# Gate groups placed between the up-projection tiles of PEER from tile 60 on, with its routing run first

## What is computed

```python
def peer(x, w_query, sub_keys, expert_u, expert_v):          # H = 8 heads, K = 16
    q = (xt @ w_query).reshape(T, H, 2, PEER_KEY_DIM // 2)
    s = jnp.einsum('thpd,hpnd->thpn', q, sub_keys)            # scores on 2 x 128 sub-keys
    sv, si = lax.top_k(s, K)
    cand = (sv[:, :, 0, :, None] + sv[:, :, 1, None, :]).reshape(T, H, K * K)
    cidx = (si[:, :, 0, :, None] * PEER_N_KEYS + si[:, :, 1, None, :]).reshape(T, H, K * K)
    best, pos = lax.top_k(cand, K)
    eidx = jnp.take_along_axis(cidx, pos, axis=-1)
    gate = jax.nn.softmax(best, axis=-1)
    a = jnp.einsum('chkd,cd->chk', expert_u[eidx], x)
    w = gate * gelu(a)
    y = jnp.einsum('chk,chkd->cd', w, expert_v[eidx])
```

## Time and profile before

| | |
|---|---|
| median of 3 runs | 2197.05 us (2192.01 to 2198.41) |
| span of the profiled execution | 2194.3 us |
| TensorE busy | 97% of the span |
| VectorE, ScalarE, GpSimd busy | 68%, 53%, 8% |
| up-projection, layer 0 | from 291.6 to 664.6 us |
| gate stage, layer 0 | from 664.6 to 746.3 us |
| down-projection, layer 0 | from 746.3 to 1097.3 us |

### The profile page before, as it was taken

One profiled execution on the slowest core, in us unless ns is written; L12 is line 12 of the kernel. 1 busy time (PEld: TensorE's weight loads), 2 busy tenths in 40 slices (PEclk: granted clock), 3 DMA queues, 4 the chain that ended last, 5 costly groups with the idle time before them and its releaser, 6 DMA issues.

```text
span 2194.3 us, 41496 instructions
## 1 busy us (share of the span) xinstructions
PE 2136.5 (97%) x14244; PEld 1917.2 (87%) x14244; DVE 1500.2 (68%) x2796; ACT 1156.8 (53%) x1835; POOL 181.5 (8%) x202
## 2 busy tenths in 40 slices
PE   8999999999999999999999999999999999999997
PEld 6987899999997788888788888999999977888886
DVE  6666767777778855555676566777777797555556
ACT  4456445544458755445444464444544596444443
POOL 1100000000007400000020000000000182000000
PEclk9999999999999999999999999999999999999999
DMA  5622455555550256666565234555555503665664
GB/s 187 198 86 88 155 165 182 182 183 183 182 180 27 59 191 193 201 203 198 160 197 167 88 106 154 166 183 183 183 183 182 166 0 101 195 201 191 200 204 134
DMA packets 97584, 350.24 MB, mean 160 GB/s; under 512 B 11312, under 2 KB 11344, under 8 KB 97520
## 3 DMA queue, kind: packets, MB, share of 16 engines
q1 hardware_dynamic: 94320, 338.69, 48.3%
q0 software_dynamic: 3200, 10.66, 1.6%
HBM read 348.26 MB, written 1.05 MB: 159 GB/s over the span
## 4 chain that ended last, share of the span: by engine, by line
PE 85%; DMA 4%; DVE 4%; ACT 2%; issue 2%; POOL 1%; POOLq 0%; DVEq 0%; SPq 0%; ACTq 0%
PE wide L1536 33%; PE acc L1521 13%; PE acc L1522 13%; PE acc L1523 13%; PE acc L2003 4%; DMA raw<-in_front 2%; DMA raw<-in_peer_v 2%; PE tr L1714 1%; POOL hot_i L574 1%; ACT hot_i L844 1%; PE acc L1874 1%; ACT hi L601 1%; PE acc L1876 1%; PE acc L1875 1%; PE wide L1972 1%
## 5 line engine op out<-in xcount | busy, mean ns | idle before, releaser
L601 ACT ACTIVATE hi<-raw 128x1024 fp32r<-128x1024 f32 (+1 forms) x644 | 676.3, 1051 | 540.7 <-DMA raw<-in_peer_v 341.9
L919 DVE TENSOR_TENSOR lo<-raw,hi 128x1024 fp32r<-128x1024 f32 x520 | 636.8, 1225 | 448.6 <-ACT hi L601 445.6
L1521 PE MATMUL acc<-xT_hi,lo 128*128 128x256 f32 x2544 | 724.9, 285 | 5.9 <-DVE kr L1132 3.2
L1522 PE MATMUL acc<-xT_lo,hi 128*128 128x256 f32 x2544 | 721.1, 283 | 0.0
L1523 PE MATMUL acc<-xT_hi,hi 128*128 128x256 f32 x2544 | 721.0, 283 | 0.0
L1521 PEld LDWEIGHTS acc<-xT_hi,lo 128*128 128x128 f32 x2544 | 489.4, 192 | 12.6 <-issue 4.6
L1522 PEld LDWEIGHTS acc<-xT_lo,hi 128*128 128x128 f32 x2544 | 489.6, 192 | 0.0
L1523 PEld LDWEIGHTS acc<-xT_hi,hi 128*128 128x128 f32 x2544 | 489.5, 192 | 0.0
L1536 PE MATMUL wide<-hi,w_lo 128*128 128x512 f32 x1016 | 313.9, 390 | 5.4 <-DVE w_lo L1462 5.2
L1536 PE MATMUL wide<-lo,w_hi 128*128 128x512 f32 x1016 | 312.9, 389 | 0.0
L1536 PE MATMUL wide<-hi,w_hi 128*128 128x512 f32 x1016 | 312.8, 389 | 0.0
(11 more groups left out here) (307 smaller groups left out, 1943.2 us busy)
## 6 DMA issues: line engine op xcount, KB each, us to landing
raw<-in_peer_u SPq DMA_DIRECT2D x256, 512.0 KB, 3.5
raw<-in_peer_v SPq DMA_DIRECT2D x254, 512.0 KB, 3.5
raw<-in_front SPq DMA_DIRECT2D x114, 512.0 KB, 3.5
ln_par<-in_ln POOLq DMA_DIRECT2D x10, 512.0 KB, 5.6
raw<-in_front SPq DMA_DIRECT2D x12, 384.0 KB, 3.2
w<-in_cmp_w POOLq DMA_DIRECT2D x16, 256.0 KB, 4.3
raw<-in_front SPq DMA_DIRECT2D x8, 312.0 KB, 3.4
xs<-in_x SPq DMA_DIRECT2D x2, 512.0 KB, 4.6
```

The costliest lines, as they stand in the source:

```text
L601: nc.scalar.activation(hi[:, s, :width], raw[:, s, :width], ACT.Identity).then_inc(hi_done, 1)
L919: nc.vector.tensor_tensor(lo[:, s], raw[:, s], hi[:, s].bitcast(F32), ALU.subtract).then_inc(lo_done, 1)
L1521: mm(dst, lo[:, s, c], xh[:, k], start=k == 0, stop=False)
L1522: mm(dst, hi[:, s, c], xl[:, k], start=False, stop=False)
```

## The change

The gate stage is taken apart and laid into the second half of the up-projection. `G0` is 60.

- TensorE runs tiles 0 to 59, with the transposes of the picks after tiles 57 and 58, then for m = 0 to 63: tile 60 + m and gate group m (into `tr` instead of `acc`), then tiles 124 to 127. `apart_j` and `v_half` are gone.
- GpSimd makes the low parts of tiles 3 to 59 (57 tiles, 128x1024 each). Its differences are gone.
- VectorE does the 16 routing units one behind the other with nothing between (24 instructions each, as the copy of the scores into `r_s`, L1346, is gone). Then it makes the rows of groups 0 and 1 and the low parts of tiles 60 to 62. For each m it then multiplies the Gelu of tile 60 + m into `big`, makes the rows of group m + 2 (8 instructions of 128x128, with iota against the token's pick), multiplies the gates of group m into all of `big`, and makes the low part of tile 63 + m.
- ScalarE writes the Gelu of tiles from 60 on into two buffers (`acts`), and fills the part of `big` behind tile 59 with ones in 34 pieces: one after each of the tiles 8 to 33, 36, 37, 40, 41, 44, 45, 56 and 57. The pieces at 36, 40 and 44 lie over the scores and wait for routing unit 4, 8 and 12 to be done. After tile 56 it waits for the end of the routing and takes the exponential of the gates.

The core of the diff:

```diff
@@ gpsimd
-                def differences(i, e):
-                    ...
+                for k in range(POOL_FIRST, G0):
+                    n = T_U + k
+                    s = n % SLOTS
+                    pool.wait_ge(hi_done, l * NT + n + 1)
+                    nc.gpsimd.tensor_tensor(lo[:, s], raw[:, s], hi[:, s].bitcast(F32), ALU.subtract).then_inc(pool_lo, 1)
@@ scalar
+                def gelu_tile(k):
+                    n = T_U + k
+                    tile_used(l, n // SLOTS, n % SLOTS)
+                    if k < G0:
+                        dst = big[:, k // JB, :, k % JB]
+                    else:
+                        if k >= G0 + 2:
+                            act.wait_ge(tile_times, l * N_TIMES + k - G0 - 1)
+                        dst = acts[k % 2][:].rearrange("p (g t) -> p g t", t=TB)
+                    ...
+                ones_at = {8 + h: h for h in range(N_ONES - 8)}
+                for c in range(3):
+                    for half in range(2):
+                        ones_at[36 + 4 * c + half] = N_ONES - 8 + 2 * c + half
+                after_gelu(0)
+                for k in range(NKEYS):
+                    gelu_tile(k)
+                    if k > 0:
+                        after_gelu(k)
+                    if k in ones_at:
+                        if ones_at[k] >= N_ONES - 8:
+                            unit_done = 4 * ((ones_at[k] - (N_ONES - 8)) // 2 + 1)
+                            act.wait_ge(route_step, (l * 16 + unit_done) * ROUTE_STEPS)
+                        fill_ones(ones_at[k])
+                    if k == 56:
+                        act.wait_ge(best_ready, l + 1)
+                        nc.scalar.activation(picks[:, 2], picks[:, 2], ACT.Exp).then_inc(gate_exp, 1)
+                        fill_ones(N_ONES - 2)
+                    ...
@@ vector
-                after_route(0, 0)
-                route(0, 0, (1, 2, 3))
-                with dve.Fori(0, NKEYS // 8 - 2) as i:
-                    route(i + 1, i, range(4, 12))
-                route(NKEYS // 8 - 1, NKEYS // 8 - 2, range(4, 11))
+                for i in range(TT * HEADS):
+                    route(i)
+                def rows(m):
+                    if m >= 2:
+                        dve.wait_ge(gates_out, l * NG + m - 1)
+                    for r in range(4):
+                        t = 4 * m + r
+                        nc.vector.tensor_scalar(hot_i[:, m % 2, r], iota[:], picksT[:, 0, t:t + 1], None, ALU.is_equal)
+                        ins = nc.vector.tensor_scalar(hot_j[:, m % 2, r], iota[:], picksT[:, 1, t:t + 1], picksT[:, 2, t:t + 1],
+                                                      ALU.is_equal, ALU.mult)
+                    ins.then_inc(hot_ready, 1)
+                ...
+                rows(0)
+                rows(1)
+                dve.wait_ge(ones_done, (l + 1) * N_ONES)
+                for k in range(G0, G0 + AHEAD):
+                    split_of(k)
+                for m in range(NG):
+                    if m > 0:
+                        dve.wait_ge(gates_read, 2 + l * NG + m)
+                    times_tile(G0 + m)
+                    if m + 2 < NG:
+                        rows(m + 2)
+                    times_gates(m)
+                    split_of(G0 + m + AHEAD)
@@ tensor
+                def gates_of(i, e):
+                    pe_.wait_ge(hot_ready, l * NG + (i * 8 + (e + 1)))
+                    pe_.wait_ge(gates_read, l * NG + (i * 8 + (e + 1)))
+                    for r in range(4):
+                        ins = mm(tr[:, e % 2, r * P:(r + 1) * P], hot_i[:, e % 2, r], hot_j[:, e % 2, r], start=True, stop=True)
+                    ins.then_inc(gates_out, 1)
+                ...
+                for k in range(56, G0):
+                    u_tile(k)
+                    if k == 57:
+                        pe_.wait_ge(best_ready, l + 1)
+                        transpose_heads(X_PK, [picks[:, a, tt] for a in range(2) for tt in range(TT)], P)
+                    if k == 58:
+                        pe_.wait_ge(picks_ready, l + 1)
+                        transpose_heads(X_PK + 1, [picks[:, 2, tt] for tt in range(TT)], P)
+                with pe_.Fori(0, NG // 8) as i:
+                    for e in range(8):
+                        u_tile_of(i, G0, e)
+                        gates_of(i, e)
+                for k in range(G0 + NG, NKEYS):
+                    u_tile(k)
```

More of the change, by code:

```diff
@@ new lines, in fill_ones, with after_gelu @@
+                def fill_ones(half):
+                    a, part = divmod(half, 2)
+                    dst = big[:, G0 // JB + a, 32 * part:32 * part + 32].rearrange("p g j t -> p (g j t)")
+                    nc.scalar.activation(dst.rearrange("p (b i) -> p b i", i=P), iota[:].unsqueeze(1).broadcast_to([P, 4, P]),
+                                         ACT.Identity, bias=ones[:, 0:1], scale=0.0).then_inc(ones_done, 1)
+                def after_gelu(k):
+                    n = T_U + k + AHEAD
+                    split_hi(l, n // SLOTS, n % SLOTS)
@@ L1373, in route @@
-                    assert sum(map(len, stages)) == ROUTE_STEPS
-                    split_after = [round((len(stages) - 1) * (e + 0.5) / len(splits)) for e in range(len(splits))]
-                    for g, stage in enumerate(stages):
-                        for ins in stage:
-                            rt.mark(ins())
-                        for e in splits:
-                            if split_after[e - splits[0]] == g:
-                                after_route(turn, e)
-                        rt.settle()
@@ L1382, in route @@
[L1382 to L1392 removed]
+                    for p in range(2):
+                        rt.mark(nc.vector.max(r_v[:, p, 0:8], scores[p]))
@@ L1523, in columns_tile @@
                     ins = mm(dst, hi[:, s, c], xh[:, k], start=False, stop=k == DK - 1)
-                    if part is not None and k == 3:
-                        ins.then_inc(part, 1)
                 ins.then_inc(slot_free[s], 1)
@@ L1980, in _ @@
+                for k in range(8):
+                    u_tile(k)
+                with pe_.Fori(0, 6) as i:
                     for e in range(8):
-                        u_tile(i, e)
-                for e in range(8):
-                    u_tile(NKEYS // 8 - 1, e, quarter_read if e == 7 else None)
-                    if e == 4:
+                        u_tile_of(i, 8, e)
+                for k in range(56, G0):
+                    u_tile(k)
+                    if k == 57:
                         pe_.wait_ge(best_ready, l + 1)
@@ L2006, in step @@
-                def step(i, nxt, fresh=False):
-                    for e in range(HOTS):
-                        gates_of(i, e)
-                        if nxt is not None:
-                            apart_j(*nxt, e, fresh)
-                half = NG // HOTS // TT
-                step(FIRST, (0, 1))
-                with pe_.Fori(1, half - 1) as i:
-                    step(i, (0, i + 1))
-                step(half - 1, (1, 0), True)
-                with pe_.Fori(half, 2 * half - 1) as i:
-                    step(i, (1, i - (half - 1)))
```

377 lines of the change are left out of this document (127 added, 250 removed).

## The result

The changed kernel takes 2303.23 us (median of 4 runs, 2299.9 to 2306.5) against 2196.24 us beside it: ratio 1.0486, 95% interval 1.0469 to 1.0503. It is 4.9% slower. The prediction said 2280, range 2205 to 2345. The profiled execution has a span of 2304.8 us against 2194.3.

What follows compares the result with a forecast made beforehand. TensorE, 97% busy, was taken as the bound. A 66 us loss less 23.6 gained is 42.4 a layer, 85 for both: 2194.3 + 85 = 2279, 2282 with 2.75 for the median; forecast 2280 us, range 2205 to 2345.

Steps and rivals of the forecast that it cites:

- The forecast's case: Routing beside GpSimd: eight VectorE instructions a unit wait for GpSimd's whole instruction, stalling TensorE; 2280 us, chance 0.50.
- eight contenders: VectorE instructions in each routing unit, three with two SBUF inputs and five small, each waiting 0.92 us on average for GpSimd.
- The rival in which only three contend: Routing: only the instructions with two SBUF inputs wait, the five small ones don't; unit 12.6 us, about 2226 us, chance 0.20.
- the hidden routing: Rival: blocking by GpSimd is rare, routing ends at 159 us and fits behind TensorE's work; 2154 us, chance 0.12.
- The rival of unchanged gates: Gate groups each wait as before, so TensorE saves only the bf16 matmuls; 2304 us, chance 0.03.
- GpSimd's subtraction: Low parts of 128x1024 on GpSimd: 2.3 us each, with 1.7 and 2.9 as bounds.
- Routing unit: One of 16 VectorE units a layer: 9.8 us alone, 17.2 beside GpSimd through 7.4 us of waits.
- End of the routing: About 231 us after the first up-projection tile; tile 60 then starts at 240 instead of 174, losing 66 us a layer.
- TensorE's own work: First up-projection to first down-projection matmul: 368.6 + 61.4 + about 1.1 = 431.1 us a layer, against 454.7 before.
- They are level, so I charge 0: Steps beside the gates: VectorE and TensorE both need 3.84 us, so no loss; bound +17 us a layer.
- 2279 for a profiled span: Whole kernel: 2194.3 us before plus 85 for both layers, from 66 lost less 23.6 gained in each.
- The gain expected of the gates: Gates laid into the up-projection free 23.6 us of TensorE a layer, 47.2 in all, if nothing else is late.

Runs made afterwards that it cites:

- e2_psum: Changed kernel with the routing's VectorE intermediates put in PSUM or straight into picks, so none of the eight waiting instructions keeps its contending SBUF operands: 2169.1 us, ratio 0.9887.

## Why the prediction held, and where it was off

- **The forecast's case happened.** Each of the eight contenders waits at times for the rest of GpSimd's instruction, stalls near tiles 42 and 46 and behind 57. The rival in which only three contend is refuted by the changed kernel's own casts (up to 2.28 us) and by the memset run; the hidden routing by the units of 17 us. The rival of unchanged gates names 2304 us, next to what was measured; that is chance, since a gate group now costs 0.88 us and the stage without the stalls takes 432.4.
- **GpSimd's subtraction**: 2.3 us taken between 1.67 and 2.90, measured 2.41. The value between the bounds was a choice that came out well; the dense 128x256 row times four was not far above.
- **Routing unit**: alone 9.8 forecast, 9.9 to 10.3 measured; beside GpSimd 17.2 forecast, 16.9 to 17.5 in the first units. Ten units of layer 0 waited, 70 us in all, where ten with 74 were forecast. The mean was right, its parts not: the wait is not spread evenly. In the first ten units of layer 0 the last product waited 1.6 us on the mean and L1305 not at all. I read this so that each wait sets the phase at which the next instruction meets GpSimd; no run tests it.
- **End of the routing**: 231 us after the first tile forecast, 232.1 measured (last reduction L1317 from 524.81 to 525.50). Tile 60: 240 forecast, 537.17 - 293.39 = 243.8 measured. The four gaps come to 63.3 us where a loss of 66 was forecast.
- **TensorE's own work**: 431.1 us forecast for the two stages, 432.4 measured without the stalls in e2_psum. The group costs 0.88 us (3.76 - 2.88) and not 0.96, which gives 5.1 us back a layer; VectorE's longer steps take 3.7 and the wait of tile 60 for its low part 2.6. "They are level, so I charge 0" was thus right in sum only: VectorE was 0.04 us under-priced a step, TensorE 0.08 over-priced.
- **The step that failed**: "2279 for a profiled span" is 25.8 us short of 2304.8. One part, 14.8 us, is the down-projection, to which the prediction gave nothing; the diff moves two of its operands, and I didn't read it for that. The other is the up-projection stages, 46.7 and 47.4 instead of 42.4 each, 9.3 in all (1.7 us lie elsewhere). There the prediction priced the stalls by their length alone. The stage of layer 0 is 501.4 = 432.4 + 60.7 of gaps that e2_psum doesn't have + 8.3, and of these 8.3 the windows show some 6.6, and the start of tile 60 another 1.5, as matmuls at a clock that had fallen while TensorE stood still. The same 2.6 us wait before tile 60 in e2_psum, with no stall before it, leaves the clock at 1.00.
- **The gain expected of the gates** was real, and is seen once the stalls are gone: e2_psum with the addresses mended takes 46.5 us less than the kernel before, against the 47.2 us that the prediction called free. The change was held back by what it did to the routing.

## What to carry to other kernels

Work that is moved to GpSimd is not free for VectorE even where VectorE has time to spare: look for each small cast, `tensor_scalar` and two-input product on VectorE's critical chain beside it, and count for each a share of GpSimd's whole instruction, however short it is itself. If such a chain has to run beside GpSimd, keep one operand (for a cast or `tensor_scalar` the output) in PSUM; here that took the unit from 17.3 to 9.9 us with the same results, where shorter GpSimd instructions only took it to 13. And when a change re-lays SBUF, compare the addresses of the stationary operands of the stages that it doesn't touch.

## What the runs showed of the hardware

- A bitwise AND of 128x16 on VectorE can take 2.39 us instead of 0.17, about as long as the 128x1024 subtraction of GpSimd (2.40 us) behind whose start it begins. Which operands matter depends on the instruction: one with two SBUF inputs waits beside a GpSimd subtraction (it takes up to 2.14 us with 128x256 and 2.82 with 128x512) and not beside a memset (427 and 694 ns at most); a cast within SBUF waits beside both (it takes up to 2.28 and 0.95 us); with PSUM in the place of one operand, or of the output of a cast, none waits (at most 6 ns over its shortest).
- The granted clock goes from 2.4 to 1.2 GHz in a gap of TensorE: 0.58 in the window of a gap of 31.6 us, then 0.21 us between matmuls, and 0.94 over the 33.7 us behind it. Behind each of the three gaps of 8.6, 31.6 and 20.4 us the matmuls lost 2.0 to 2.6 us.
- 128x512 fp32 matmuls whose stationary operands lie at odd multiples of 64 bytes (or 32 bytes lower) take 395 ns in the rows instead of 390 at multiples of 128, some 18 us in 3048 of them. Why is open.
